# Feed-forward low halves of two units of eight: an accumulating DMA inside SBUF in place of VectorE

## What is computed

```
h2 = rms_norm(x, norm_ffn_g)
u  = square(relu(h2 @ w_up))        # 2048 -> 8192
x  = x + u @ w_down                 # 8192 -> 2048
out = rms_norm(x, norm_final_g)
```

## Time and profile before

| | |
|---|---|
| median of 3 runs | 1591.18 us (1590.75 to 1592.46) |
| span of the profiled execution, first to last instruction | 1587.2 us |
| TensorE matmul busy | 1567.3 us (99%) |
| VectorE busy | 1101.6 us (69%) |
| ScalarE busy | 739.1 us (47%) |
| GpSimd busy | 10.8 us (1%) |
| DMA | 301.40 MB, mean 190 GB/s; SyncE's queue 57.0% of 16 engines |

### The profile page before, as it was taken

The page is one execution under the profiler, slowest core; times in us unless marked ns, Lnnn a source line. Parts: engine busy times, 40 slices in busy tenths (PEclk is TensorE's granted clock), DMA queues, the critical chain, the costliest instruction groups (busy, mean ns, idle before and its releaser), DMA issues.

```text
span 1587.2 us, 18857 instructions
## 1 busy us (share of the span) xinstructions
PE 1567.3 (99%) x6992; PEld 1292.0 (81%) x6992; DVE 1101.6 (69%) x1398; ACT 739.1 (47%) x983; POOL 10.8 (1%) x17
## 2 busy tenths in 40 slices
PE   9999999999999999999999999999999999999998
PEld 7877778888888888888878888888888888888886
DVE  7877777544447776666699888458864687548855
ACT  6455555444444454444444444444444445444443
POOL 0000000000000000000000000000000000000000
PEclk9999999999999999999999999999999999999999
DMA  9645454565655555556555665565656565555562
GB/s 365 197 134 160 157 159 151 179 201 185 232 179 185 185 190 173 187 192 211 198 201 193 206 209 186 190 199 183 197 189 201 175 203 188 200 194 183 189 203 89
DMA packets 149606, 301.40 MB, mean 190 GB/s; under 512 B 4784, under 2 KB 4912, under 8 KB 149040
## 3 DMA queue, kind: packets, MB, share of 16 engines
q1 hardware_dynamic: 149120, 299.65, 57.0%
q10 hardware_dynamic: 432, 1.02, 0.2%
HBM read 298.55 MB, written 2.10 MB: 189 GB/s over the span
## 4 chain that ended last, share of the span: by engine, by line
PE 88%; DVE 8%; issue 2%; ACT 1%; DMA 0%; SPq 0%; POOLq 0%; DVEq 0%; POOL 0%; ACTq 0%
PE acc L371 85%; DVE buf L887 3%; DVE wlo L878 2%; DVE qbd L887 1%; PE sps L383 1%; PE pps L401 1%; ACT buf L591 0%; ACT whi L584 0%; DMA raw<-in_w_in 0%; PE pps L394 0%; DVE buf L1245 0%; DVE tb_lo L926 0%; DVE ta_lo L1273 0%; PE tps L427 0%; ACT prob L610 0%
## 5 line engine op out<-in xcount | busy, mean ns | idle before, releaser
L878 DVE TENSOR_TENSOR wlo<-raw,whi 128x1024 fp32r<-128x1024 f32 x544 | 662.6, 1224 | 444.9 <-ACT whi L584 442.0
L584 ACT ACTIVATE whi<-raw 128x1024 fp32r<-128x1024 f32 x544 | 573.0, 1059 | 720.5 <-PE acc L371 718.8
L371 PE MATMUL acc<-whi,ta_hi 128*128 128x512 f32 x1312 | 517.2, 394 | 2.5 <-DVE wlo L878 1.6
L371 PE MATMUL acc<-whi,ta_lo 128*128 128x512 f32 x1312 | 511.2, 390 | 0.0
L371 PE MATMUL acc<-wlo,ta_hi 128*128 128x512 f32 x1312 | 510.7, 389 | 0.0
L371 PEld LDWEIGHTS acc<-whi,ta_hi 128*128 128x128 f32 x1312 | 246.4, 188 | 55.8 <-issue 3.9
L371 PE MATMUL acc<-whi,tb_hi 128*128 128x512 f32 x736 | 287.7, 391 | 2.6 <-DVE tb_lo L926 2.6
L371 PEld LDWEIGHTS acc<-wlo,ta_hi 128*128 128x128 f32 x1312 | 246.4, 188 | 52.0 <-issue 1.7
L371 PEld LDWEIGHTS acc<-whi,ta_lo 128*128 128x128 f32 x1312 | 246.3, 188 | 51.6
L371 PE MATMUL acc<-whi,tb_lo 128*128 128x512 f32 x736 | 286.4, 389 | 0.0
L371 PE MATMUL acc<-wlo,tb_hi 128*128 128x512 f32 x736 | 286.4, 389 | 0.0
(11 more groups left out here) (128 smaller groups left out, 659.4 us busy)
## 6 DMA issues: line engine op xcount, KB each, us to landing
raw<-in_w_in SPq DMA_DIRECT2D x67, 1024.0 KB, 5.2
raw<-in_w_up SPq DMA_DIRECT2D x64, 1024.0 KB, 5.2
raw<-in_w_down SPq DMA_DIRECT2D x64, 1024.0 KB, 5.0
raw<-in_w_gate SPq DMA_DIRECT2D x32, 1024.0 KB, 5.3
raw<-in_w_att SPq DMA_DIRECT2D x16, 1024.0 KB, 5.0
raw<-in_w_ret SPq DMA_DIRECT2D x16, 1024.0 KB, 5.0
raw<-in_w_out SPq DMA_DIRECT2D x16, 1024.0 KB, 5.1
xt<-in_x_t SPq DMA_DIRECT2D x8, 256.0 KB, 8.8
```

What stands on the lines that cost most here:

```text
L371: last = nc.tensor.matmul(acc[B.parity][:, t, :], a[:, k, tok], b[:, slot, :], start=(k == 0 and n == 0), stop=(k == KCH - 1 and n == 2))
L584: nc.scalar.activation(whi[:, s:s + UCH, :], raw[:, u * UCH:(u + 1) * UCH, :], ACT.Copy).then_inc(hi_ready, 1)
L878: V_.tensor_tensor(wlo[:, s:s + UCH, :], raw[:, u * UCH:(u + 1) * UCH, :], whi[:, s:s + UCH, :].bitcast(f32), ALU.subtract).then_inc(lo_re ...
```

## The change

In blocks 37 to 67 the low halves of units 6 and 7 no longer come from VectorE. ScalarE writes the negated raw weights of both units, rounded, into a new tile `low4` (4 chunks of 128x512, 1 MB, placed where `qbd`, `decay` and `ptr` lay in earlier stages). Then GpSimd's queue issues a DMA from `raw` to `low4` with an add: `low4 = raw - rounded(raw)`. ScalarE still makes `whi` for both units. TensorE waits at units 6 and 7 for the DMA (`low_full`) and for `hi_ready`, and multiplies by `low4`. SyncE's load of quarter 3 of the next block waits for the DMA and for ScalarE's unit 7 where it waited for VectorE's unit 7. `lo_ready` counts six units a block from block 37 on. There is one `low4`; `negated` waits for TensorE to have finished the block before.

```diff
--- before.py
+++ after.py
@@ -69,9 +69,18 @@
         self.turn = j * (step // 2) + first // 2
         self.reused = first >= 2
         self.very_first = first == 0
+        self.ffn = first >= FFN
+        self.follows = first > FFN or (first == FFN and later(j))
+        self.before = j * step + (first - 1 - FFN)
 
     def unit(self, u):
 
+        return self.number * UNITS + (u + 1)
+
+    def low(self, u):
+
+        if self.ffn:
+            return self.number * DVE_UNITS + (u + 1 + FFN * (UNITS - DVE_UNITS))
         return self.number * UNITS + (u + 1)
 
 
@@ -104,6 +113,8 @@
 
 
 LAST = 68
+FFN = 37
+DVE_UNITS = 6
 
 ACT_COLS, DVE_COLS = 768, 640
 WARM_UP = 16
@@ -187,6 +198,7 @@
         decay = place("decay", [P, RET_HEADS, RET_COLS], f32, at_c + 16 * K)
         ptr = place("ptr", [P, 2, RET_COLS], f32, at_c + 28 * K)
         final = place("final", [P, TILES, D], f32, at_c)
+        low4 = place("low4", [P, (UNITS - DVE_UNITS) * UCH, COLS], f32r, at_c + 16 * K)
         kT = place("kT", [P, KV_HEADS, S], f32, at_m)
         vwin = place("vwin", [P, 3, KV_HEADS, P], f32, at_m + 4 * K)
         prob = place("prob", [P, 4, P], f32, at_m + 10 * K)
@@ -204,6 +216,7 @@
 
         raw_full = [sem(f"raw_full{s}") for s in range(LOADS)]
         hi_ready, lo_ready, unit_done = sem("hi_ready"), sem("lo_ready"), sem("unit_done")
+        low_set, low_full = sem("low_set"), sem("low_full")
         evacuated = [sem("evacuated0"), sem("evacuated1")]
         xt_full = [sem(f"xt_full{u}") for u in range(UNITS)]
         first_full, x_full = sem("first_full"), sem("x_full")
@@ -268,7 +281,13 @@
                 sp.lower_ap_dma(src)
                 if not B.very_first:
 
-                    sp.wait_ge(lo_ready, B.number * UNITS + (2 * s + 2 - UNITS))
+                    if not B.ffn or not B.follows:
+                        sp.wait_ge(lo_ready, B.number * UNITS + (2 * s + 2 - UNITS))
+                    elif s < DVE_UNITS // 2:
+                        sp.wait_ge(lo_ready, (B.before + FFN) * DVE_UNITS + (2 * s + 2 + FFN * (UNITS - DVE_UNITS)))
+                    else:
+                        sp.wait_ge(low_full, B.before * 16 + 16)
+                        sp.wait_ge(hi_ready, B.number * UNITS)
                 sp.dma_start(raw[:, GCH * s:GCH * (s + 1), :],
                              src).then_inc(raw_full[s], 16)
 
@@ -362,13 +381,19 @@
                 for u in range(u0, u1):
                     if u == 0 and B.reused:
                         pe.wait_ge(evacuated[B.parity], B.turn)
-                    pe.wait_ge(lo_ready, B.unit(u))
+                    by_dma = B.ffn and u >= DVE_UNITS
+                    if by_dma:
+                        pe.wait_ge(low_full, B.before * 16 + 32)
+                        pe.wait_ge(hi_ready, B.unit(u))
+                    else:
+                        pe.wait_ge(lo_ready, B.low(u))
                     for kk in range(UCH):
                         k, slot = u * UCH + kk, (u * UCH + kk) % (KCH // 2)
+                        low = low4[:, k - DVE_UNITS * UCH, :] if by_dma else wlo[:, slot, :]
                         for t in range(TILES):
                             tok = slice(t * P, (t + 1) * P)
-                            for n, (a, b) in enumerate(((hi, whi), (hi, wlo), (lo, whi))):
-                                last = nc.tensor.matmul(acc[B.parity][:, t, :], a[:, k, tok], b[:, slot, :],
+                            for n, (a, b) in enumerate(((hi, whi[:, slot, :]), (hi, low), (lo, whi[:, slot, :]))):
+                                last = nc.tensor.matmul(acc[B.parity][:, t, :], a[:, k, tok], b,
                                                         start=(k == 0 and n == 0), stop=(k == KCH - 1 and n == 2))
                     last.then_inc(unit_done, 1)
 
@@ -583,6 +608,13 @@
                     s = u * UCH % (KCH // 2)
                     nc.scalar.activation(whi[:, s:s + UCH, :], raw[:, u * UCH:(u + 1) * UCH, :],
                                          ACT.Copy).then_inc(hi_ready, 1)
+
+            def negated(B):
+
+                if B.ffn:
+                    act.wait_ge(raw_full[LOADS - 1], B.number * 16 + 16)
+                    act.wait_ge(unit_done, B.number * UNITS)
+                    nc.scalar.activation(low4[:], raw[:, DVE_UNITS * UCH:KCH, :], ACT.Copy, scale=-1.0).then_inc(low_set, 1)
 
             def scaled(B, dst, func, scale):
 
@@ -803,6 +835,7 @@
                     if j == 1:
                         act.wait_ge(t_full, T_STAGE4 + 4)
                     residual_squares(Block(B5 + j - 1), j - 1, x1_sq)
+                negated(B)
                 split(B, 5, 7)
                 if j == 0:
                     hi_from_turned(T_STAGE4 + 3, tc_hi, 3)
@@ -816,6 +849,7 @@
                 if not first:
                     split(B[0], 0, 5)
                     residual_squares(Block(B6 - 1, 8, q), 3, down_sq)
+                    negated(B[0])
                     split(B[0], 5, 8)
                 for i in range(1, 5):
                     split(B[i], 0, 4)
@@ -824,6 +858,7 @@
                     else:
                         act.wait_ge(t_full, q * 4 + (T_STAGE6 + i - 1))
                     scaled_relu(B[i - 1])
+                    negated(B[i])
                     split(B[i], 4, 8)
                     hi_from_turned(q * 4 + (T_STAGE6 + i - 1), tb_hi, i - 1)
                 for i in range(5, 8):
@@ -872,7 +908,7 @@
 
             def split(B, u0, u1):
 
-                for u in range(u0, u1):
+                for u in range(u0, min(u1, DVE_UNITS) if B.ffn else u1):
                     dve.wait_ge(hi_ready, B.unit(u))
                     s = u * UCH % (KCH // 2)
                     V_.tensor_tensor(wlo[:, s:s + UCH, :], raw[:, u * UCH:(u + 1) * UCH, :],
@@ -1318,6 +1354,12 @@
                 nc.gpsimd.tensor_tensor(powr[:].rearrange("p i t -> p (i t)"), msq[:], mhalf[:], ALU.pow).then_inc(rpow_ready, 1)
             pool.wait_ge(ms2_ready, 1)
             nc.gpsimd.tensor_tensor(rstd2[:], msq[:, 0:2], mhalf[:, 0:2], ALU.pow).then_inc(rstd2_ready, 1)
+            def lows(n):
+                pool.wait_ge(low_set, n + 1)
+                pool.dma_start(low4[:].bitcast(f32), raw[:, DVE_UNITS * UCH:KCH, :], accum_op=ALU.add).then_inc(low_full, 16)
+
+            for n in range(LAST - FFN):
+                lows(n)
             for t in range(TILES):
                 pool.wait_ge(ms3_ready, t + 1)
                 nc.gpsimd.tensor_tensor(rstd3[:, t:t + 1], msq[:, t:t + 1], mhalf[:, t:t + 1], ALU.pow).then_inc(rstd3_ready, 1)
```

## The result

The changed kernel takes 1595.98 us (1595.51 to 1598.49, 4 runs) against 1590.97 us: a ratio of 1.0036, interval 1.0023 to 1.0049. (The median of the kernel before now has a fourth run in it, 1588.99 us.) It is slower, by 5.0 us where 21.5 were forecast. The profiled execution spans 1593.7 us, 6.5 more than the 1587.2 of the earlier trace rows.

What follows compares the result with a forecast made beforehand. TensorE, busy 99% of the span, was taken as the bound. Removing four stalls (-4.0 us) and adding transfer stalls (+25.5) gave +21.5: span 1608.7, time 1612.7 us, range 1585.5 to 1700.

Steps and rivals of the forecast that it cites:

- The sign: Whole kernel: the change was forecast slower, by 21.5 us; chance of slower 0.60.
- X: Issue-to-landing time of one 1 MB DMA transfer with add: 8.0 us alone, 11.0 in residual blocks.
- the free queue: POOL's queue: nothing else stands between its two rstd steps, so the 31 transfers find it free.
- The bound and the gain: TensorE is 99% busy; only the four waits for tb_lo, 1.0 us a group, can go: -4.0 us.
- relu block: Blocks 1 to 4 of a group, 16 in all: slack 12.1 us, X 9 to 10, no stall.
- T: Time in a block where TensorE finishes the block before; it comes to unit 6 at T + 16.3.
- the load beside the transfer: Residual blocks: quarter 2's load falls into the transfer and takes 3.0 us of the engines, making X 11.0.
- residual block: Blocks 5 to 7, first of a later group, and 37; 15 in all: slack 9.3 us, stall 1.7 each.
- the 25.5 us of stalls: TensorE waiting for the transfer at unit 6 of 15 residual blocks, 1.7 us each.
- The price of lateness: Late transfers at unit 6: 15 us for each us of X above 9.3, 16 more above 12.1.
- it fits everywhere: Rival, all blocks: X stays under 9.3 us, only the four stalls go, 1587.2 us; chance 0.28.
- The time around the span: Outside the profiled execution: median 1591.2 against span 1587.2, so 4.0 us added to the forecast span.

Runs made afterwards that it cites:

- The order-only kernel: Kernel before, no DMA: in blocks 1 to 4 of a group VectorE does the last transposes ahead of unit 6's split; 1585.45 us, ratio 0.9976.
- the run with the late copy: Changed kernel with the first transfer early, but the negated copy behind unit 6's split in 15 residual blocks; 1635.23 us, ratio 1.0276.
- the kernel with the first transfer ahead: Changed kernel with the first transfer queued on POOL ahead of the wait for the second norm's mean square; 1586.08 us, ratio 0.9980.

## Why the prediction was wrong

The sign was right by luck: the slowdown does not come from where I put it, it is a quarter of the size, and without its one cause, which no rival named, the same change is 0.2% faster than the kernel before. Two steps failed, the size of X and the free queue. By its steps:

- **The bound and the gain** held. TensorE's four waits for `tb_lo` went, and nothing else was won. ScalarE's copy took 1.91 us (1.94 estimated). In relu block 3 of group 1 the last eight transposes now run in one piece, and `tb_lo` ends at 1144.11, T + 15.6 with T = 1128.55, which is what was forecast (1157.2 - 1141.64). By time, ScalarE's unit 3, then VectorE:

```profile
1128.55 1.06 ACT L609 ACTIVATE whi<-raw 128x1024 fp32r<-128x1024 f32 x1 [1.66 <-PE acc L396]
...
1138.16 3.59 DVE L923 STREAM_TRANSPOSE buf<-buf 32x256 f32<-32x256 f32 x8
1142.88 1.23 DVE L962 TENSOR_TENSOR tb_lo<-buf,tb_hi 128x1024 fp32r<-128x1024 f32 x1 [1.13 <-ACT tb_hi L628]
```

  The order-only kernel, which keeps only that step, has all of it: from block 37's last unit to the last block it takes 658.57 us, where the kernel before took 1557.98 - 895.56 = 662.42. Block 37's `ta_lo` wait stayed, as said.
- **The step that failed first is the size of X**, and in it the load beside the transfer. Alone I had 8.0 us, and 7.1 was measured in block 37. For the load I added its whole 3.0 us and got 11.0; measured 8.1, so the load's term was 1.0. (The relu blocks, for which I had 9 to 10, took 7.8 to 9.8 us, most of them near 8.1.) The view of DMA queues from 1179.2 to 1187.3 us, a residual block of the changed kernel, shows who gave way (packets, MB, share of 16 engines; then KB and time to landing):

```profile
q0 software_dynamic: 144, 1.05, 74.4%
q1 hardware_dynamic: 143, 0.29, 9.6%
...
low<-raw POOLq DMA_DIRECT2D x1, 1024.0 KB, 8.1
raw<-in_w_down SPq DMA_DIRECT2D x1, 1024.0 KB, 8.8
```

  Here the load pays: it goes out 1.9 us behind the transfer (1181.11 and 1179.18), moves 0.29 of its 1 MB while the transfer runs, and lands after 8.8 us instead of the 5.1 that the same quarter took before. It had 10 us to spare by my own count. So the 25.5 us of stalls shrank to one wait of 0.5. This is no rule for every meeting: with the copy earlier, where a load was out 0.8 us before the transfer, the transfer took 10.4 us, near my 11.0. Who goes out first differs between the two; no run tests that by itself. The price of lateness, had it come, lacked the clock: I let a late block cost its wait alone, and in the run with the late copy 8 of 15 blocks cost 1.7 us more.
- **The step that was wrong outright** is the sentence "POOL has nothing else between its two rstd steps, so its queue is free". Between them, yes. But block 37's transfer is wanted before the first of them has run. The waits of the kernel before had a row for it:

```profile
POOL rstd L1320 <- DVE msq L1215: 282.6, 1, 282.6
```

  I read that as an idle engine. It was a queue closed until VectorE had made `msq`, and VectorE makes it right behind the `ta_lo` of the earlier trace rows. I counted what stood behind each added wait on TensorE and ScalarE and did not ask, for the first transfer, what stood ahead of it. The stop of 8.2 us and the slow clock behind it are the whole loss.
- **The rival "it fits everywhere"**, at 0.28, is what the 30 other blocks did. It is the kernel with the first transfer ahead, 0.9980. I had it right in mechanism and let the load beside it decide against it.
- **The time around the span** was mixed from two things: the median of the runs and the span of one execution. For the changed kernel's profiled execution both are known, 1595.5 and 1593.7, so 1.8 us lie around it and not 4.0.

## What to carry to other kernels

Before a new instruction is put on an idle engine's queue, read what that queue is waiting for at the first time it is needed; a long wait in the profile is a closed door, not free room, and the first iteration is where it shows. Before work is taken off an engine, find the one instance that stands on the critical path, and try to move it behind what is waited for: here that alone gave all of the gain. When a DMA meets another one, ask which of them gives way and whether that one has slack, and do not charge the whole meeting to the urgent one unread: here the load gave way to the transfer that went out before it, and the transfer gave 2.3 us where a load was out first.

## What the runs showed that I had not expected

- A POOL transfer and a SyncE load that meet do not share evenly, and not always the same one gives way. Transfer out 1.9 us before the load: 8.1 us for 7.1 alone, and the load 8.8 for 5.1. Load out 0.8 us before the transfer: the load 6.0, the transfer 10.4.
- A stop of TensorE of as little as 2.1 us was followed by matmuls at half clock (0.64 over the next 4.7 us) and cost 1.7 us more than itself, and another of 2.1 us in the same execution was not (1.00); behind the stop of 8.6 us in the changed kernel the clock cost 1.4, behind one of 9.1 us 2.4. In these the price of the clock does not follow the length of the stop.
- The add in flight: 2.6 us per MB above a plain copy inside SBUF, 5.7 us for a second MB with it.
